# Two-block model on one Trainium2 core: alternating gate and value tiles in the second block's input projection, and a 31-tap convolution on VectorE alone

## The reference, cut to what matters

```
def fourier_conv_mixer(h, w_in, conv_w, conv_b, conv_g, w_out):
    p = h @ w_in                                            # 1024 -> 512 + 512 + 512
    pa, pu, pg = jnp.split(p, [A_WIDTH, A_WIDTH + B_WIDTH], axis=-1)
    fa = pa.reshape(b, L, A_GROUPS, A_GROUP_DIM)
    ya = jnp.fft.fft2(fa, axes=(1, 3), norm='ortho').real.reshape(b, L, A_WIDTH)
    u = pu * jax.nn.sigmoid(pg)                             # value times gate
    u = depthwise_conv(u, conv_w, 31 taps, padding 15) + conv_b
    yb = jax.nn.silu(rmsnorm(u, conv_g))
    return jnp.concatenate([ya, yb], axis=-1) @ w_out
```

## Time and profile before

| | us |
|---|---|
| median of 3 runs | 2548.87 (2546.36 to 2554.71) |
| the profiled execution's own time | 2545.8 |
| its span in the trace | 2544.0 |
| TensorE, mean granted clock over the span | 0.947 of full speed |

### The profile page before, as it was taken

The page is one execution under the profiler, slowest core; times in us unless marked ns, Lnnn a source line. Parts: engine busy times, 40 slices in busy tenths (PEclk is TensorE's granted clock), DMA queues, the critical chain, the costliest instruction groups (busy, mean ns, idle before and its releaser), DMA issues. The chain is left out here.

```text
span 2544.0 us, 27421 instructions
## 1 busy us (share of the span) xinstructions
PE 2153.0 (85%) x10514; PEld 1375.9 (54%) x10514; DVE 826.4 (32%) x1726; ACT 388.4 (15%) x726; POOL 114.2 (4%) x56
## 2 busy tenths in 40 slices
PE   7899998988999792888988898986988787888884
PEld 6788886667888540544444444444646433333332
DVE  3456662136666527032111111113173211111112
ACT  3311111122111301320000000002122000000000
POOL 0000000000000009300000000001000000000000
PEclk9999999999999896989999999997989999999997
DMA  7556665303765732016999999976121699999993
GB/s 255 198 197 216 248 231 195 136 33 124 252 218 205 285 138 99 1 66 250 397 397 396 396 396 397 397 280 246 66 99 67 232 397 396 396 396 397 397 397 142
DMA packets 273636, 638.07 MB, mean 251 GB/s; under 512 B 7120, under 2 KB 10224, under 8 KB 273456
## 3 DMA queue, kind: packets, MB, share of 16 engines
q1 hardware_dynamic: 256096, 595.48, 63.0%
q0 software_dynamic: 5600, 21.27, 2.3%
q10 hardware_dynamic: 11888, 20.62, 2.2%
HBM read 606.41 MB, written 30.93 MB: 251 GB/s over the span
## 5 line engine op out<-in xcount | busy, mean ns | idle before, releaser
L680 PE MATMUL T<-ring,S 128*64 128x512 f32 x2112 | 486.9, 614 | 77.4 <-issue 69.6
L680 PEld LDWEIGHTS T<-ring,S 128*64 128x64 f32 x2112 | 178.7, 142 | 378.1 <-issue 375.0
L561 PE MATMUL T<-X,ring 128*128 128x256 f32 x1536 | 340.1, 381 | 0.0
L561 PEld LDWEIGHTS T<-X,ring 128*128 128x128 f32 x1536 | 293.5, 192 | 40.3 <-issue 0.6
L699 PE MATMUL T<-ring,S 128*64 128x512 f32 x1056 | 241.2, 597 | 40.2 <-DVE S L1479 40.2
L1477 DVE TENSOR_TENSOR S<-S,T 128x256 f32<-128x256 f32 x66 | 27.8, 422 | 727.4 <-ACT S L1061 727.4
L1281 DVE SCALAR_TENSOR_TENSOR S<-ring,cs,S 128x512 f32<-128x512 f32 x336 | 229.6, 747 | 0.0
L659 PEld LDWEIGHTS T<-S 128*128 128x128 f32 x1696 | 196.8, 196 | 41.2 <-issue 41.2
L659 PE MATMUL T<-S 128*128 128x128 f32 x1696 | 203.4, 281 | 14.3 <-DVE S L1360 14.3
L569 PE MATMUL T<-S,ring 128*128 128x256 f32 x768 | 176.7, 383 | 15.8 <-DVE S L1311 15.8
L569 PEld LDWEIGHTS T<-S,ring 128*128 128x128 f32 x768 | 143.6, 190 | 51.3 <-DVE S L1311 33.1
(11 more groups left out here) (269 smaller groups left out, 1555.4 us busy)
## 6 DMA issues: line engine op xcount, KB each, us to landing
ring<-in_exp_w_gate SPq DMA_DIRECT2D x66, 2048.0 KB, 18.6
ring<-in_exp_w_up SPq DMA_DIRECT2D x66, 2048.0 KB, 22.7
ring<-in_exp_w_down SPq DMA_DIRECT2D x66, 2048.0 KB, 19.9
ring<-in_ffn_w_up SPq DMA_DIRECT2D x24, 2048.0 KB, 12.7
ring<-in_mod_w SPq DMA_DIRECT2D x24, 2048.0 KB, 7.9
ring<-in_ffn_w_down SPq DMA_DIRECT2D x12, 2048.0 KB, 7.9
y_rows<-S ACTq DMA_DIRECT2D x132, 128.0 KB, 5.5
y_rows<-zb POOLq DMA_DIRECT2D x4, 3072.0 KB, 22.6
```

The lines of the kernel that those rows point to most:

```text
L561: ins = pe.matmul(T[:, m % 2, h * S:(h + 1) * S], w[:, k, m * P:(m + 1) * P], x1[:, k, :], start=(k == 0), stop=(k == KT - 1))
L680: ins = pe.matmul(T[c * B:(c + 1) * B, s, :].rearrange("p (a n) -> p a n", a=2), xgT[:, k, s * B:(s + 1) * B], ring[:, 3 * s:3 * s + 2, k ...
```

## The change

TensorE runs gate and value units in turn (gate 0, value 0, gate 1, ...), waiting for both weight chunks ahead of the first; the Fourier units stay last. The units at which the slots of the three chunks come free become 6, 7 and 11 of the projection. VectorE convolves all four channel tiles: `gated(m)` waits for value tile m and multiplies it by its gate, then 16 turns follow, each with one tap of tile m's first 16 and one of tile m - 1's last 15; a fifth round ends tile 3 alone. The last tap of each tile counts `yc_ready` up, and the squares wait for their own pair of tiles. ScalarE makes no products, and GpSimd's additions are gone. On TensorE the norm's sums now stand behind tile 1 of `out_ab`'s first half, and its spread behind tile 2.

```diff
@@ SyncE's release of the weight slots
-        last_unit.update({c0["in_ab"] + j: u0["in_ab"] + 4 * j + 3 for j in range(3)})
+        last_unit.update({c0["in_ab"] + j: u0["in_ab"] + (6, 7, 11)[j] for j in range(3)})
@@ TensorE
-            def norm(r, k_tiles=KT, n=N2, sq=S1, off=0):
+            def norm_sums(r, k_tiles=KT, n=N2, sq=S1, off=0):
                 for k in range(k_tiles):
                     if k % 2 == 0:
                         pe.wait_ge(n_sq, nsq0[r] + k // 2 + 1)
                     ins = quarter_sums(sq[:, off + k, 0:n], n, k == 0, k == k_tiles - 1)
                 ins.then_inc(n_ms, 1)
+
+            def norm_spread(r, n=N2):
                 pe.wait_ge(n_rs, r + 1)
                 spread(n).then_inc(n_bc, 1)
...
-            for j in range(3):
-                c = c0["in_ab"] + j
-                landed(c)
-                dense(c, 4, lambda k: H[:, k, :], u0["in_ab"] + 4 * j, N2, ready=(h_ready, 0) if j == 0 else None)
+            c, u = c0["in_ab"], u0["in_ab"]
+            landed(c)
+            landed(c + 1)
+            for m in range(4):
+                for j in range(2):
+                    dense(c + j, 1, lambda k: H[:, k, :], u + 2 * m + j, N2, m0=m,
+                          ready=(h_ready, 0) if m + j == 0 else None)
+            landed(c + 2)
+            dense(c + 2, 4, lambda k: H[:, k, :], u + 8, N2)
...
             for m in range(4):
                 take(pe, u + m)
                 out_ab(m, range(4))
-            norm(1, 4, sq=S1, off=4)
+                if m == 1:
+                    norm_sums(1, 4, sq=S1, off=4)
+                if m == 2:
+                    norm_spread(1)
@@ ScalarE
-                evac(u0["in_ab"] + m, S1[:, 4 + m, :], func=ACT.Sigmoid)
-            def conv_products(taps):
...
+                evac(u0["in_ab"] + 2 * m, S1[:, 4 + m, :], func=ACT.Sigmoid)
-                conv_products(range(5 * m, 5 * m + 5))
...
-                conv_products(range(20 + 2 * g, 22 + 2 * g))
...
-                conv_products(range(28 + g, min(29 + g, CONV)))
-            norm(1, S3, 4, sq=S1, off=4, wait=lambda k: act.wait_ge(yc_ready, 2))
+            norm(1, S3, 4, sq=S1, off=4, wait=lambda k: act.wait_ge(yc_ready, k + 1))
@@ VectorE
-            for m in range(4):
-                u = u0["in_ab"] + 4 + m
+            last = {}
+
+            def gated(m):
+                u = u0["in_ab"] + 2 * m + 1
                 got(dve, u)
-                read(dve, u0["in_ab"] + m)
+                read(dve, u - 1)
                 ins = V.tensor_tensor(U[:, m, :, PADC:PADC + S], pair(u),
                                       S1[:, 4 + m, :].rearrange("p (a n) -> p a n", a=2), ALU.mult)
                 ins.then_inc(free[u % 4], 1)
-            read(dve, u)
-            last = {}
-            for t in range(CONV):
-                for m in range(3):
...
+                read(dve, u)
+
+            def tap(m, t):
+                y = S3[:, m, :].rearrange("p (a n) -> p a n", a=2)
+                w = vc("conv_w", 4 * t + m)
+                if t == 0:
+                    ins = V.tensor_scalar(y, U[:, m, :, 0:S], w, vc("conv_b", m), ALU.mult, ALU.add)
+                else:
+                    own.wait(last[m])
+                    ins = STT(out=y, in0=U[:, m, :, t:t + S], scalar=w, in1=y, op0=ALU.mult, op1=ALU.add)
+                if t < CONV - 1:
                     last[m] = own.mark(ins)
-            for m in range(3):
-                own.wait(last[m])
-            dve.sem_inc(yc_ready, 1)
+                else:
+                    ins.then_inc(yc_ready, 1)
+
+            half = (CONV + 1) // 2
+            for m in range(5):
+                if m < 4:
+                    gated(m)
+                for t in range(half):
+                    if m < 4:
+                        tap(m, t)
+                    if m > 0 and half + t < CONV:
+                        tap(m - 1, half + t)
@@ GpSimd
-            for t in range(1, CONV):
-                pool.wait_ge(cv_ready, t + 1)
-                ins = pool.tensor_tensor(S3[:, 3, :], S3[:, 3, :], S3[:, 4 + t % 4, :], ALU.add)
...
```

More of the change, by code:

```diff
@@ L320, in build @@
         ln_rs, ln_bc, n_rs, n_bc = sem("ln_rs"), sem("ln_bc"), sem("n_rs"), sem("n_bc")
-        cv_ready, cv_used = sem("cv_ready"), sem("cv_used")
         yc_ready, yn_ready, yb_ready = sem("yc_ready"), sem("yn_ready"), sem("yb_ready")
@@ L605, in norm @@
                 ins.then_inc(n_ms, 1)
+            def norm_spread(r, n=N2):
                 pe.wait_ge(n_rs, r + 1)
                 spread(n).then_inc(n_bc, 1)
+            def norm(r, k_tiles=KT, n=N2, sq=S1, off=0):
+                norm_sums(r, k_tiles, n, sq, off)
+                norm_spread(r, n)
             def route(l):
@@ L1611, in _ @@
                 ins.then_inc(free[u % 4], 1)
-            read(dve, u)
-            last = {}
-            for t in range(CONV):
-                for m in range(3):
[L1616 to L1620, removed]
-                        own.wait(last[m])
-                        ins = STT(out=y, in0=U[:, m, :, t:t + S], scalar=w, in1=y, op0=ALU.mult, op1=ALU.add)
-                    last[m] = own.mark(ins)
-            for m in range(3):
-                own.wait(last[m])
-            dve.sem_inc(yc_ready, 1)
+                read(dve, u)
[8 more added lines that the diff above has]
+                if t < CONV - 1:
+                    last[m] = own.mark(ins)
+                else:
[9 more added lines that the diff above has]
+                        tap(m - 1, half + t)
             dve.wait_ge(n_std, 2)
```

## The result

The median is 2488.43 us (2484.63 to 2490.81), that of the kernel before, run beside it, 2550.68 (2546.36 to 2554.71): 62.3 us less, a ratio of 0.9751 with a 95% interval of 0.9731 to 0.9772. Forecast were 2486 us and a gain of 61.6.

What follows compares the result with a forecast made beforehand. TensorE bounds the kernel, with a 49.36 us hole traced to a GpSimd addition stalled beside VectorE's taps. Gains of 48.6 + 8.3 + 1.8 + 2.9 = 61.6 us gave 2484.2 profiled, 2487.3 as median, stated as 2486; range 2479 to 2497.

Steps and rivals of the forecast that it cites:

- The four terms of the sum: TensorE's gains at the wait before `dft1`, in `dft1`, in `dft2` and around the norm: 48.6 + 8.3 + 1.8 + 2.9 = 61.6 us.
- 48.6 us for the wait: TensorE ahead of `dft1`: last Fourier tile copied at 967.9, so `dft1` starts at 968.6 instead of 1017.24.
- 8.3 + 1.8 for the Fourier products: TensorE at full clock: `dft1` 7.7 us instead of 16.0, `dft2` 14.8 instead of 16.6.
- The rival with the low clock: TensorE's clock stays low in `dft1` and `dft2`: up to 20 us lost, half likelier, so 2496 us; chance 0.07.
- 2.9 for the norm: `out_ab`'s first half and norm on TensorE: 16.1 instead of 19.0 us, from the three idle times around the norm.
- VectorE from 899 to 989, 89.8 us: VectorE's gate products and 124 taps: 0.783 us a serial tap, 0.663 interleaved, ending at about 989.
- Banks: PSUM banks freed for Fourier units 1 and 3 by gate products 2 and 3: no wait, closest 4.7 us to spare.
- The rival of a pacing VectorE: Projection: all taps at 0.783 us, TensorE waits 2.7 us at Fourier unit 3; time 2489 us; chance 0.07.
- No loss in the experts: Experts' loop: starts about 61.6 us earlier, lasts as long as before, can't give the gain back.

Runs made afterwards that it cites:

- the PSUM run: Kernel before, with VectorE's 90 taps taking their second input from a PSUM bank instead of the running sum in SBUF: 2500.52 us, ratio 0.9795.
- the run with only the norm split: Kernel before, with only the norm's sums and spread moved behind tiles 1 and 2 of the output projection's first half: 2549.35 us, ratio 0.9983.
- The run with long rounds: Changed kernel, with all 31 taps of a tile in its own round, each waiting for the one before: 2505.75 us, ratio 0.9819.
- idle additions from the norm of x on: Changed kernel, with 30 additions that nothing needs on GpSimd from the end of the norm of x on: 2504.85 us, ratio 0.9808.
- taps tile by tile: Kernel before, with all 31 taps of tile 0, then 1, then 2, each waiting for the one before: 2533.38 us, ratio 0.9922.
- the run with the norm whole: Changed kernel, with the norm's sums and spread back behind all four first halves of the output projection: 2493.29 us, ratio 0.9768.

## Why the prediction was right

The place and the cause were read from four rows that point at each other: TensorE waits for a copy, the copy stands behind a product, the product waits for an addition, the addition lasts 54 us, as long as VectorE's taps. That this was VectorE's doing was argued there from the ends, 1.1 us apart; the PSUM run shows it.

The four terms of the sum were 61.6 us and came out at 61.5 by trace. The two profiled executions lie only 57.3 us apart, and the medians 62.3, so that the forecast lies within 2.4 us of the measured median is in part luck; the terms are not.

- *48.6 us for the wait*: 48.7. It hung on ScalarE's list being free of waits only.
- *8.3 + 1.8 for the Fourier products*: 8.0 + 1.7. The rival with the low clock fell: 1.00 throughout, also in `dft1`'s short groups. Only `dft2`'s 1.7 us are slow rows regained. `dft1`'s rows were slow too before (6.68 us for the first 16), but that cost nothing there: in the run with only the norm split they took 5.10, and the next rows began 7.00 us after the first in both, when ScalarE's copy came from behind its products. `dft1`'s 8.0 us are those products, which ScalarE no longer makes.
- *2.9 for the norm*: 3.1, twice. It was taken from two idle times (1.38 + 1.50), though the prediction speaks of three. The slow rows that can stand behind them, 1.6 us, had no term; in the profile that it was read from there were none.
- *VectorE from 899 to 989, 89.8 us*: 88.8 (902.98 to 991.74), at 0.788 us a serial tap ((11.78 - 0.75) / 14) and 0.663 interleaved; the interleaved round took 21.06 us. By the rule of the Trainium skill that the next operation does not start until the pipeline is empty ("VectorE: DVE Perf Modes", section "The DRAIN you can't avoid") no two taps could start closer than one lasts, 0.743; the interleaved rows do, as in before.
- *Banks*: no wait; 5.2 us to spare, forecast 4.7. The rival of a pacing VectorE was charged its wait of 2.7 us alone. The run with long rounds is another schedule (its gate product 3 comes some 11 us later than that rival's), but there a wait of 2.4 us cost 1.6 more in slow rows behind it, which the rival's price leaves out.
- *No loss in the experts*: the loop's window is nearly the same, and it starts 59.1 us earlier. From there to the end it took 1387.0 us, inside the 1384.8 to 1389.1 of all thirteen profiles.

Too small to settle are the 4.2 us by which the span differs in parts that the change does not touch (2.3 ahead of the projection, 1.4 in it, 1.8 from the loop on, less 1.2 between); the runs of the kernel before differ by 8 us among themselves.

## What to carry to other kernels

Look for one instruction whose time is far above the median of its line, and for the stream on the other engine that ended with it. A helper engine that stands still beside a dense stream does nothing for it, and its queue carries the wait to engines that need neither; work given to it should be such that nobody's list stands behind it. When TensorE's output feeds a long chain elsewhere, order the units so that the chain begins with the first pair, and check each bank's release against the longer of the two rounds. Charge a wait on TensorE also with the slow rows behind it.

## What the runs showed of the hardware that was not expected

- GpSimd's additions (1.27 us alone) and VectorE's two-input taps (0.747) alternate at 1.67 us a pair, 0.35 less than their sum; both rows grow (1.54 to 1.6 and 1.64 us).
- A dense stream of taps holds an addition for as long as it lasts (16.9, 54.0 and 71.3 us), but only one that arrives in it; one that was there first keeps its turn, whether two or four chains are interleaved.
- A tap that reads its second input from PSUM takes 0.740 us beside additions of 1.27: neither slows the other.
- Tap 0, a `tensor_scalar` with one SBUF tensor, is held up too: 1.56 us beside additions (idle additions from the norm of x on) and 1.48 (taps tile by tile), against 0.55 alone. The gate product, with one input in PSUM and one in SBUF, took 0.68 to 0.69 with additions and without.
- TensorE's granted clock, 1.00 ahead of them, was 0.64 and 0.50 in the windows behind waits of 2.4 and 9.3 us in the run with long rounds and 0.55 behind idle times of 1.4 and 1.5 us in the run with the norm whole, and it stayed at 1.00 behind the same two in the profile of before and behind those of 0.69, 0.78 and 0.89 us in the changed kernel.
